# Seven block products for each pair of f tiles in the prompt's down projection, and weight sums made ahead by GpSimd and kept in DRAM

## What is computed

```python
x = x + concat(diff_attention(h), gqa_attention(h)) @ w_out
x = x + cross_attention(rmsnorm(x), rmsnorm(mem)) @ w_xo
h = rmsnorm(x)
u = h @ w_up                                    # width 2 * 2816
u = u[t-1] * conv_w[0] + u[t] * conv_w[1] + u[t+1] * conv_w[2] + conv_b
a, b = split(u)
x = x + (silu(a) * b) @ w_down                  # w_down: 2816 x 1024
y = rmsnorm(x)
```

## Time and profile before

| | us |
|---|---|
| median of 3 runs (2412.42 to 2413.26) | 2412.44 |
| span of the profiled execution | 2409.6 |
| PE busy | 2357.1 (98%), 12306 matmuls |
| DVE busy | 1691.7 (70%) |
| GpSimd busy | 1393.2 (58%) |
| ACT busy | 1013.6 (42%) |
| DMA | 260.40 MB, mean 108 GB/s |
| granted TensorE clock, mean | 0.996 |

### The profile page before, as it was taken

The page is one execution under the profiler, slowest core; times in us unless marked ns, Lnnn a source line. Parts: engine busy times, 40 slices in busy tenths (PEclk is TensorE's granted clock), DMA queues, the critical chain, the costliest instruction groups (busy, mean ns, idle before and its releaser), DMA issues.

```text
span 2409.6 us, 34258 instructions
## 1 busy us (share of the span) xinstructions
PE 2357.1 (98%) x12306; PEld 2018.2 (84%) x12306; DVE 1691.7 (70%) x2509; ACT 1013.6 (42%) x2045; POOL 1393.2 (58%) x1601
## 2 busy tenths in 40 slices
PE   7999999999999989999999999999999999999998
PEld 6999888888998878888888888888878888888886
DVE  7537777788889964244333388877688888888887
ACT  4436655555668852133232212211243333333334
POOL 5454645588877730053230267767777777777775
PEclk9999999999999999999999999999999999999999
DMA  8743434432212063132244422222421111111112
GB/s 295 250 172 142 158 132 158 166 132 98 94 63 84 13 178 115 53 115 78 96 149 135 145 105 96 91 103 99 146 79 62 53 53 55 55 53 53 53 53 92
DMA packets 102727, 260.40 MB, mean 108 GB/s; under 512 B 10144, under 2 KB 45344, under 8 KB 92064
## 3 DMA queue, kind: packets, MB, share of 16 engines
q1 hardware_dynamic: 101264, 257.82, 30.8%
q10 hardware_dynamic: 1296, 0.39, 0.1%
HBM read 209.95 MB, written 48.23 MB: 107 GB/s over the span
## 4 chain that ended last, share of the span: by engine, by line
PE 57%; DVE 3%; POOL 1%; ACT 1%; issue 1%; DMA 1%; DVEq 0%; POOLq 0%; SPq 0%; ACTq 0%
PE r_bank L2104 27%; PE r_bank L2010 11%; PE r_bank L1981 10%; PE r_bank L2043 5%; PE r_bank L2062 1%; PE r_bank L2091 1%; DVE r_conv L2477 1%; PE r_bank L2025 1%; PE r_bank L2074 0%; DVE r_x_p L2665 0%; DMA r_rows_w<-in_w_up_units 0%; DVE r_x_p L2682 0%; POOL r_s_lo L1849 0%; ACT r_conv L2314 0%; DVE r_x_p L2555 0%
## 5 line engine op out<-in xcount | busy, mean ns | idle before, releaser
L843 PE MATMUL t_proj<-t_w_hi,t_hbuf 128*128 128x384 f32 x1056 | 312.3, 349 | 1.9 <-ACT t_nat L994 0.7
L2555 DVE TENSOR_TENSOR r_x_p<-r_bank,r_x_p 128x512 f32<-128x512 f32 x320 | 208.4, 683 | 49.3 <-PE r_bank L2104 48.2
L2477 DVE SCALAR_TENSOR_TENSOR r_conv<-r_rows,r_taps,r_conv 128x511 f32<-128x511 f32 (+3 forms) x134 | 181.1, 1352 | 48.0 <-ACT r_conv L2314 45.5
L1153 DVE TENSOR_REDUCE t_max_neg<-t_scores 128x1 f32<-128x1024 f32 (+1 forms) x192 | 197.0, 1038 | 23.5 <-PE t_scores L877 18.1
L1017 ACT ACTIVATE t_prob<-t_scores,t_max_neg 128x1024 f32<-128x1024 f32 (+1 forms) x192 | 187.3, 977 | 50.0 <-DVE t_max_neg L1153 45.7
L843 PEld LDWEIGHTS t_proj<-t_w_hi,t_hbuf 128*128 128x128 f32 x1056 | 195.5, 189 | 8.1 <-issue 6.8
L1026 ACT CAST t_pt_hi<-t_turn 128x512 fp32r<-128x512 f32 x240 | 140.1, 586 | 107.6 <-PE t_turn L896 83.4
L1173 DVE TENSOR_TENSOR t_pt_lo<-t_turn,t_pt_hi 128x512 fp32r<-128x512 f32 x240 | 163.5, 686 | 30.0 <-ACT t_pt_hi L1026 26.3
L843 PE MATMUL t_proj<-t_w_lo,t_hbuf 128*128 128x384 f32 x528 | 178.4, 338 | 0.0
L1776 POOL TENSOR_TENSOR r_stat<-r_stat,minus_half 128x1 f32<-128x1 f32 x24 | 14.1, 587 | 275.0 <-DVE r_stat L2440 275.0
L1831 POOL TENSOR_TENSOR r_w_lo<-r_stage,r_w_hi 128x1024 fp32r<-128x1024 f32 (+1 forms) x86 | 166.2, 1932 | 7.2
(11 more groups left out here) (307 smaller groups left out, 7272.5 us busy)
## 6 DMA issues: line engine op xcount, KB each, us to landing
t_hbuf<-split_x SPq DMA_DIRECT2D x60, 1024.0 KB, 4.8
r_stage<-in_w_up_units SPq DMA_DIRECT2D x44, 512.0 KB, 3.2
r_rows_w<-in_w_up_units SPq DMA_DIRECT2D x88, 256.0 KB, 3.1
split_x<-t_hbuf SPq DMA_DIRECT2D x12, 1024.0 KB, 5.3
r_stage<-in_w_down SPq DMA_DIRECT2D x22, 512.0 KB, 3.2
r_wd_raw<-in_w_down SPq DMA_DIRECT2D x42, 256.0 KB, 2.6
t_stage<-in_w_in_units SPq DMA_DIRECT2D x6, 1536.0 KB, 6.5
t_xkv_raw<-in_w_xkv_heads SPq DMA_DIRECT2D x16, 512.0 KB, 6.3
```

The source lines that it names most:

```text
L843: ins = nc.tensor.matmul(proj_bank(i), l, r[:, k, :], start=(k == 0 and j == 0), stop=(k == KT - 1 and j == 2))
L1153: nc.vector.tensor_reduce(max_neg[:, n % COLS:n % COLS + 1], ps_s[:, n % 2, 0:p.keys], AX.X, ALU.max, negate=True).then_inc(max_done, 1)
L2477: return nc.vector.scalar_tensor_tensor(out, src, tap_of(j, s, i), out, ALU.mult, ALU.add)
L2555: nc.vector.tensor_tensor(x_p[:, t, cols], down_bank(n), x_p[:, t, cols], ALU.add).then_inc(p_add, 1)
```

## The change

**Downs.** f tiles 0 to 19 are taken in ten pairs. For a pair the down projection is seven products of 512 tokens x 512 columns with sums of blocks (`DOWNS`: p7, p4, p1, p6, p5, p3, p2), each four token tiles of three matmuls: 28 downs a pair in place of 32. Sixteen of them are woven into tile 2m+2 and twelve into tile 2m+3. Tile 1 carries none now, tile 21 twelve. A left operand is a sum of quarters of the gated activations (`a_sums` on GpSimd, four a pair), its high part is cast on ACT (`a_high`), its low part made on DVE (`a_low`), seven of each a pair. The last two f tiles are done as before.

**Weight sums.** The sums s1 to s4 of each f tile's w_up quarters and four sums of each pair's w_down quarters are no longer made in the last stage. In the planned stages, at due times 13.2 us apart, a group is loaded (four DMAs of 256 KB), summed (four `block_sum` on GpSimd) and stored to DRAM (four DMAs): 22 + 10 groups. The last stage loads each operand straight into its slot (`load_operand`), and a down's weight into a ring of three slots.

**Orders.** SP, ACT, GpSimd and DVE have new orders in the last stage.

```diff
-def operand_orders():
-    sums, low = [("s2a", 0), ("s2", 0), ("s1", 0), ("s3", 0), ("s4a", 0), ("s4", 0)], [("w11", 0), ("s2", 0), ("s1", 0)]
...
+PAIRS = (FT - 2) // 2
+SUMMED = FT + PAIRS
+DOWNS = ("p7", "p4", "p1", "p6", "p5", "p3", "p2")
+ND, FIRST_DOWNS = len(DOWNS), 16
+LEFT = {"p7": "s3", "p4": "a22", "p1": "a11", "p6": "s2", "p5": "s1", "p3": "s4", "p2": "a12"}
+DOWN_WEIGHT = {"p7": "t3", "p4": "t4", "p1": "b11", "p6": "t2", "p5": "t1", "p3": "b22", "p2": "b21"}
...
+    for z in range(SUMMED):
+        b = 6 + 13.2 * z
+        put("SP", b, 1.0, "block_load", (z,), ("block_store", (z - 2,)) if z >= 2 else None)
+        for n in range(4):
+            put("POOL", b + 8 + 1.4 * n, 1.3, "block_sum", (z, n), ("block_load", (z,)), ("block_sum", (z, n - 1)) if n else None)
+        put("SP", b + 17, 1.0, "block_store", (z,), ("block_sum", (z, 3)))
...
             sp.dma_start(gain_s[:, :], a["final_norm_g"].partition_broadcast(P)).then_inc(s_gain, 16)
-            for t in range(PTILES):
-                sp.dma_start(x_p[:, t, :], x2[t * P:(t + 1) * P, :]).then_inc(p_rows_loaded, 16)
-            for name in ("w11", "w21", "w22", "w12"):
-                load_rows(1, name)
             for i in range(FT):
...
+                if more:
+                    for name in ("w11", "s2", "s1"):
+                        load_operand(i + 1, name)
+                load_operand(i, "s4")
+                if i == 0:
+                    send_sample(0)
+                    for t in range(PTILES):
+                        sp.dma_start(x_p[:, t, :], x2[t * P:(t + 1) * P, :]).then_inc(rows_loaded, 16)
...
+            def a_sums(m, name):
+                if name == "s3":
+                    pool.wait_ge(late_prod, 2 * m + 1)
+                    pool.wait_ge(*((pair_down, pair_at(m - 1, "p1")) if m else (y_sent, 16 * ST)))
...
-                        elif 0 < i < LAST and o >= 3:
-                            prompt_down(i - 1, HK * (o - 3) + k)
+                        elif i > 1 and i % 2 == 0 and o >= 3:
+                            prompt_down(i // 2 - 1, HK * (o - 3) + k)
+                        elif i > 1 and i % 2 and o >= 3 and k:
+                            prompt_down(i // 2 - 1, FIRST_DOWNS + 3 * (o - 3) + k - 1)
...
-                    pe.wait_ge(p_add, P_DOWNS * (LAST - 1))
+                    pe.wait_ge(p_add, PAIR_DOWNS * PAIRS)
...
-                    gated_low(i - 1, edge, edge_hi, edge_split)
...
                 if i == 1:
+                    dve.wait_ge(row_rstd, 2)
+                    sample_scale(2)
+                    sample_scale(3)
+                    dve.wait_ge(rows_loaded, 16 * (ST + PTILES))
```

681 lines of the change are left out of this document (400 added, 281 removed).

## The result

The changed kernel takes 2419.66 us, median of 7 runs (2417.58 to 2422.15), the kernel before 2412.44 in the same seven rounds. The ratio is 1.0031, with an interval of 1.0021 to 1.0041: slower by 0.3%. The profiled execution has a span of 2416.2 us against 2409.6. The time of a run is 1.8 us more than its span (2418.03 for the profiled one).

The account below looks back on a forecast made before the run. PE was taken as the bound, its time in steady prompt tiles being the number of matmuls. 2412.44 − 27.2 (matmuls) + 17.8 (entry) + 5.8 (end) + 1.0 (middle stages) = 2409.8 us, "no change"; range 2398 to 2421.

Parts of the forecast that it names:

- Matmuls, −27.2: Steady prompt tiles: 120 matmuls fewer over ten pairs, at 0.2267 us each, save 27.2 us.
- I take no loss: 0 to +3: Steady tiles: other engines keep up with PE, tightest at down p6; no loss taken, bounds 0 to +3 us.
- The middle stages, +1.0 (0 to +4): 32 groups put in between 880 and 1310: rstd sometimes waits for one GpSimd sum, costing 1.0 us.
- the 0.7 us of room: Middle stages: the gap between the end of DVE's norm (927.39) and the start of PE's transposes (928.09).
- rstd behind whole groups: Slower rival, middle stages: the norm waits for chained sums or late group loads, up to 4.5 us a tile; chance 0.17.
- DMA in the middle, up to 2.5 us a load: Middle stages: a load behind four of the groups' new loads lands up to 2.5 us later.
- The entry, +17.8: Tiles 0 to 2: s3(1) lands behind x_p's 4.2 MB, delaying w12(1), s4(1) and w11(2); costs 17.8 us.
- The rival that the small loads pass: Entry: x_p's drain does not hold tile 1; entry −1.6 us, time 2390; chance 0.08.
- The end, +5.8: After the last product: the first end half waits for all 280 adds, plus lower clock; costs 5.8 us (4.1 to 7).
- the forecast's own: The prediction's main case, the sum of its own terms: 2406 to 2415 us, chance 0.47.

Follow-up runs that it names:

- m_none: Changed kernel without the 32 groups of block loads, sums and stores; the last stage loads plain weight quarters: 2409.06 us.
- m_dma: Changed kernel with the groups' loads and stores kept but GpSimd's 128 block sums left out: 2409.36 us.
- m_dve: Changed kernel with the 128 block sums made by DVE in place of GpSimd, placed anew by the planner: 2414.67 us.
- m_lead: Changed kernel with the planner told that group loads land 6 us later and a sum takes 1.8 us, so sums stand elsewhere: 2420.26 us.
- e_spread: Changed kernel with x_p's eight loads spread singly between operand loads of tiles 1 and 2, and the first pair's weight load three loads later: 2410.93 us.
- c_five: e_spread plus value_whole(0) ahead of high(1, s3), first a_sums behind s4(1)'s low, and DVE's last pair-down adds ahead of add_s4: 2399.49 us.
- e_late: Changed kernel with the eight x_p loads moved behind the load of w12(1), three operand loads later: 2414.86 us.
- m_gp: Changed kernel with GpSimd's 128 sums kept on two blocks loaded once, other group loads and all stores left out: 2430.16 us.

## Why the prediction was wrong, point by point

- **Matmuls, −27.2**: right. 12186 in all, and w11(2) to w11(21) is 24.4 us shorter for 108 matmuls less, 0.226 us each; by the 215.7 ns of the Trainium skill (TensorE: Matmul & The Clock Gate, on the back-to-back gap) it would be 23.3. "I take no loss: 0 to +3" holds at +1.8: the odd tiles are full, the even ones, in which the forecast saw the tightest wait, take 0.2 us more each than their 132 matmuls, with no single wait over 0.3 us; where it comes from was not traced.
- **The middle stages, +1.0 (0 to +4)**: the step that failed; it measured 9.7. The step put a rstd behind one sum at a time, "waits at most 1.3, of which 0.6 reaches PE". The trace has the rstd 3.0 to 5.5 us late in four tiles, behind two or three sums, GpSimd's own wait for a block load, or splits that were pushed back. A second cost was not in the step at all: a norm beside GpSimd's sums takes 2.3 us in place of 1.28, and that 1.0 alone is more than the 0.7 us of room. That GpSimd's sums are the cause is shown by m_none, m_dma and m_dve: 9.7 us with the sums on GpSimd, 1 without them, 5.2 with them on DVE. How the 9.7 us split between the late rstd and the longer steps of DVE stays open: each of these runs takes away both, m_lead has the rstd on time in 23 of 24 tiles and is no faster, and by the lengths of the norms the changed kernel's waits are mainly the late rstd's. The price stood in the rival "rstd behind whole groups" (up to 4.5 a tile, chance 0.17), which has the first cost and not the second; it hits five tiles, not 24. (Its threshold was worked out loosely: 7.5 us over 24 tiles are 0.31 each, not 0.35.) The rule named beside it (the Trainium skill, GPSIMD Engine Reference, specifications: interfaces shared with VectorE) agrees with this trace: the norm of 1024 columns, with its two inputs in SBUF, takes 2.3 us with a sum beside it and 1.28 without; m_dma, without sums, has no norm over 1.7 us. The forecast named it and gave it no term.
- **DMA in the middle, up to 2.5 us a load**: m_dma shows about 1 us for all 67 MB.
- **The entry, +17.8**: right in its links, and nearly in its sum. The forecast's term has 19.2 to w11(2) and −1.4 in tile 2; they measured 20.4 and −1.7, together 18.7. x_p's issue to s3(1) at ACT 14.7 us (16.2 forecast), w12(1) 50.8 us after w11(0) (54.1 forecast), s4(1) 66.4 (66.2), w11(2) 70.7 (69.5). That s4(1) comes when it was said to is in part luck: w12(1) is 3.3 us earlier than forecast and the way from there to s4(1) as much longer. The rival that the small loads pass has no support: in every kernel with the drain in one piece something behind it waited. How it splits: of 20.4 us more than before, e_spread takes 9.6 off by SP's queue alone, and the orders of ACT and GpSimd another 7 (c_five); what stays is 3.8 lost more than before.
- **The end, +5.8**: 3.7. From the last product to the end of the span are 5.7 us more than before, 0.7 of them three matmuls of the last down; so the part that the step describes is 5.1. The wait is 4.62 where PE was said to start 5.2 after the product, and the lower clock level follows it; the two waits that tile 21 had before (0.21 and 0.64, 1.4 us lost in all) are gone, since its products are now stretched by downs. That was not in the step.
- **Sum**: 2407.0 of span was forecast and 2416.2 came: +8.7 in the middle, +0.9 in the entry, +1.8 in the steady tiles, −2.1 at the end. The other 0.6 is that the profiled run stands 1.6 us under the median. The measured 2419.66 lies inside the range of 2398 to 2421, but by the slower rival's mechanism and not by the forecast's own (2406 to 2415, "no change").

## What to carry to other kernels

An engine's free time is no room if the work that is put there stands in one queue with a short step that another engine waits for: ask not how busy the engine is but what waits behind the longest chain of it, its own waits for DMA included. Ask too what the work does to the engine beside it: DVE's norm took 1.8 times as long beside GpSimd's sums. In every kernel here with x_p's 4.2 MB in one piece, something that came behind it waited, operand or store, and moving it whole only changed which; issuing it piece by piece between the small ones took 9.6 of the 20.4 us off. Where SP waited in its queue for a store to land, everything behind was late by that store's place in the drain (8.6 us in e_late).

## What the runs showed of the hardware that was not expected

- The same 128 sums of 128x512 took 1399 ns on GpSimd and 766 on DVE, and a DVE step with two inputs in SBUF was longer beside GpSimd's two-input ones: the norm of 1024 columns 2.3 us against 1.28 alone, the low part of 1024 columns 2.1 against 1.22. In six traces (before, changed, m_dma, m_gp, m_lead and m_dve) no norm without GpSimd beside it took over 1.3 us.
- With 4 MB under way the queues moved 420 GB/s and a load of 256 KB behind them took 9.7 us from issue to its reader; the median of 256 KB loads of w_up to their landing was 3.1 in the kernel before.
